# Seven half-width products in place of eight in four down projections of a two-block transformer kernel

## The reference, cut to what matters

```
# block 1
f = rmsnorm(h, norm_ffn_g)
h = h + (silu(f @ w_gate) * (f @ w_up)) @ w_down          # w_down: 2816 x 1024
# block 2
u = causal_dwconv(h2 @ w_ff_up, conv_ff_w, conv_ff_b)      # three taps, per channel
gate, val = split(u, 2)
x = x + (silu(gate) * val) @ w_ff_down                     # w_ff_down: 2816 x 1024
```

## Time and profile before

| | before |
|---|---|
| median of 3 runs | 1555.33 us (1553.41 to 1555.92) |
| span of the profiled execution, first to last instruction | 1553.9 us |
| TensorE matmul busy | 1539.9 us (99%), 7847 matmuls |
| VectorE busy | 747.5 us (48%) |
| ScalarE busy | 395.1 us (25%) |
| GpSimd busy | 905.7 us (58%) |
| mean granted TensorE clock | 0.999 |

### The profile page before, as it was taken

One profiled execution on the slowest core, in us unless ns is written; L12 is line 12 of the kernel. 1 busy time (PEld: TensorE's weight loads), 2 busy tenths in 40 slices (PEclk: granted clock), 3 DMA queues, 4 the chain that ended last, 5 costly groups with the idle time before them and its releaser, 6 DMA issues.

```text
span 1553.9 us, 22779 instructions
## 1 busy us (share of the span) xinstructions
PE 1539.9 (99%) x7847; PEld 1291.7 (83%) x7847; DVE 747.5 (48%) x1157; ACT 395.1 (25%) x757; POOL 905.7 (58%) x536
## 2 busy tenths in 40 slices
PE   8999999999999999999999999999999999999998
PEld 7779999988888888888888888777877888888887
DVE  4157840232335354742343245868567751552456
ACT  4221210233442012210010013456564320220122
POOL 5645556544445667766666666653454666666653
PEclk9999999999999999999999999999999999999999
DMA  6223333322223432333333333322222323333322
GB/s 213 82 72 91 85 93 91 86 68 59 64 68 104 147 95 82 108 94 95 100 100 98 95 88 102 93 70 64 60 67 82 94 81 108 96 98 103 95 81 95
DMA packets 266712, 142.67 MB, mean 92 GB/s; under 512 B 6445, under 2 KB 263749, under 8 KB 266389
## 3 DMA queue, kind: packets, MB, share of 16 engines
q1 hardware_dynamic: 265285, 139.16, 30.5%
q10 hardware_dynamic: 1360, 2.56, 0.4%
HBM read 137.38 MB, written 4.19 MB: 91 GB/s over the span
## 4 chain that ended last, share of the span: by engine, by line
PE 95%; DVE 3%; ACT 1%; issue 1%; DMA 0%; ACTq 0%; DVEq 0%
PE PS L645 74%; PE PS L643 12%; PE PS L872 1%; PE PS L849 1%; PE PS L957 1%; PE PS L797 1%; DVE BL L2051 1%; PE PS L875 0%; PE PS L923 0%; PE PS L848 0%; PE PS L862 0%; DVE L L1881 0%; PE PS L1003 0%; DVE L L1864 0%; ACT SBX L1422 0%
## 5 line engine op out<-in xcount | busy, mean ns | idle before, releaser
L586 POOL TENSOR_TENSOR WL<-RAW,WH 128x1024 fp32r<-128x1024 f32 (+1 forms) x259 | 622.7, 2404 | 21.6
L584 POOL TENSOR_SCALAR WH<-RAW 128x1024 fp32r<-128x1024 f32 (+1 forms) x259 | 280.4, 1083 | 607.6 <-DMA RAW<-in_w_in_dram 257.5
L645 PE MATMUL PS<-BH,WH 128*128 128x512 f32 x928 | 366.6, 395 | 1.2 <-DVE BL L2051 1.1
L645 PE MATMUL PS<-BL,WH 128*128 128x512 f32 x928 | 361.4, 389 | 0.0
L645 PE MATMUL PS<-BH,WL 128*128 128x512 f32 x928 | 361.1, 389 | 0.0
L645 PEld LDWEIGHTS PS<-BH,WH 128*128 128x128 f32 x928 | 174.2, 188 | 42.4 <-issue 4.4
L645 PE MATMUL PS<-AH,WH 128*128 128x512 f32 x528 | 205.9, 390 | 0.0
L645 PE MATMUL PS<-AL,WH 128*128 128x512 f32 x528 | 205.4, 389 | 0.0
L645 PE MATMUL PS<-AH,WL 128*128 128x512 f32 x528 | 205.4, 389 | 0.0
L645 PEld LDWEIGHTS PS<-BH,WL 128*128 128x128 f32 x928 | 174.3, 188 | 37.2 <-issue 1.7
L645 PEld LDWEIGHTS PS<-BL,WH 128*128 128x128 f32 x928 | 174.2, 188 | 36.6
(11 more groups left out here) (334 smaller groups left out, 1817.4 us busy)
## 6 DMA issues: line engine op xcount, KB each, us to landing
RAW<-in_w_in_dram SPq DMA_DIRECT2D x89, 512.0 KB, 3.4
RAW<-in_w_ff_up_dram SPq DMA_DIRECT2D x44, 512.0 KB, 3.6
RAW<-in_w_gate_dram SPq DMA_DIRECT2D x22, 512.0 KB, 3.6
RAW<-in_w_up_dram SPq DMA_DIRECT2D x22, 512.0 KB, 3.6
RAW<-in_w_down_dram SPq DMA_DIRECT2D x16, 512.0 KB, 3.6
RAW<-in_w_ff_down_dram SPq DMA_DIRECT2D x16, 512.0 KB, 3.6
RAW<-in_w_out_dram SPq DMA_DIRECT2D x10, 512.0 KB, 3.7
RAW<-in_w_conv_out_dram SPq DMA_DIRECT2D x8, 512.0 KB, 3.7
```

What stands on the lines that cost most here:

```text
L584: nc.gpsimd.tensor_scalar(WH[:, slot, 0:kc], RAW[:, slot, 0:kc], 1.0, 1.0, ALU.mult, ALU.mult).then_inc(w_hi, 1)
L586: nc.gpsimd.tensor_tensor(WL[:, slot, 0:kc], RAW[:, slot, 0:kc], WH[:, slot, 0:kc].bitcast(F32), ALU.subtract).then_inc(w_ready, 1)
L645: last = mm(bank_of(name, i)[0:rows], w[:, w_at, k, 0:rows], a[:, k, :], start=st, stop=sp_)
```

## The change

It touches `dn0`, `dn1`, `ed0` and `ed1`. Two panels of 8 k and 512 positions are treated as a 2 x 2 block product: the weights are the even and odd k of the first and of the second panel, the activations the even and odd k in the first and second half of the positions (256 columns each). Such a block product can be made of seven block products (Winograd's form of Strassen's method) with sums of the weights and of the activations in front and sums of the results behind. A stage is four such pairs; `product(name, n, q)` is product q of pair n: 4 k x 3 passes = 12 matmuls of 256 columns.

- TensorE: products in the order 1, 5, 2, 6, 4, 7, 3 (`DUO_ORDERS`), the first pair by `duo_stage`: 1, 5, then three of the four k of 2, 6, 3, 4, then their last k, then 7. Products 1, 6 and 7 accumulate in one bank, and VectorE must have read the bank (`evict`) before the next of them starts. `EARLY_PARTS` is 3.
- VectorE: sums of activations while the hidden tiles are made (`even_piece`, `odd_pieces`) and their low parts; three weight sums (`add_second`), a fourth (`add_third`), the low part of the second panel (`low_second`), and seven additions to `H` per pair (`evict`) in place of two. Its order at the end of a gate/up stage is `first_duo`, then `later_duos`.
- ScalarE: all high parts of weights and weight sums, and of the activation pieces.
- GpSimd: per pair the low part of the first panel (`low_first`, 1024 elements per partition), of the first two weight sums (`low_sums`, 1024) and of the third (`low_third`, 512), in the order of `duo_lows`. It makes no high parts in these stages.
- Some per-norm semaphores become one each, and one memset (`XA`) moves to `gu2`.

```diff
+DUO_ORDERS = [(1, 5, 6, 2, 3, 4, 7)] + [(1, 5, 2, 6, 4, 7, 3)] * (DUOS - 1)
+EARLY_PARTS, MADE = 3, 12
 # GpSimd
+            def low_first(name, n):
+                m, s = duo(name, n), duo_slots(name, n)[0]
+                pool.wait_ge(first_hi, m + 1)
+                nc.gpsimd.tensor_tensor(WAL[:, n % 2], RAW[:, s], WH[:, s].bitcast(F32), ALU.subtract).then_inc(first_lo, 1)
+            def low_sums(name, n):
+                pool.wait_ge(duo_added, 4 * duo(name, n) + 4)
+                pool.wait_ge(sums_hi, duo(name, n) + 1)
+                nc.gpsimd.tensor_tensor(WSL[:, n % 2, 0:2], WS[:, n % 2, 0:2], WSH[:, 0:2].bitcast(F32), ALU.subtract).then_inc(sums_lo, 1)
+            def duo_lows(name):
+                low_first(name, 0)
+                low_sums(name, 0)
+                low_third(name, 0)
+                low_first(name, 1)
+                low_sums(name, 1)
+                low_third(name, 1)
+                low_first(name, 2)
+                low_sums(name, 2)
+                low_first(name, 3)
+                low_third(name, 2)
+                low_sums(name, 3)
+                low_third(name, 3)
...
 # TensorE
+            def product(name, n, q, ks=range(4)):
...
+                if ks[0] == 0:
+                    if q in (1, 2):
+                        pe.wait_ge(first_lo, m + 1)
+                    elif q in (5, 6):
+                        pe.wait_ge(sums_lo, m + 1)
+                    elif q == 3:
+                        pe.wait_ge(third_lo, m + 1)
+                    else:
+                        pe.wait_ge(second_lo, m + 1)
+                    if q == 6:
+                        pe.wait_ge(duo_out, 7 * m + DUO_ORDERS[n].index(1) + 1)
+                    elif q == 7:
+                        pe.wait_ge(duo_out, 7 * m + DUO_ORDERS[n].index(6) + 1)
...
+                pe.wait_ge(pieces_lo, MADE * DUO_STAGES.index(name) + 3 * ks[-1] + ARRIVAL[q])
+                for k in ks:
+                    rh, rl = A7H[:, k, PIECES[q]], A7L[:, k, PIECES[q]]
+                    for i, (w, a) in enumerate(((hi, rh), (lo, rh), (hi, rl))):
+                        last = mm(bank, w[:, k], a, start=k == 0 and i == 0 and q not in (6, 7), stop=k == 3 and i == 2, skip_group_check=True)
+            def duo_stage(name):
+                early, rest = range(EARLY_PARTS), range(EARLY_PARTS, 4)
+                product(name, 0, 1)
+                product(name, 0, 5)
+                for q in (2, 6, 3, 4):
+                    product(name, 0, q, early)
+                for q in (6, 2, 3, 4):
+                    product(name, 0, q, rest)
+                product(name, 0, 7)
+                for n in range(1, DUOS):
+                    for q in DUO_ORDERS[n]:
+                        product(name, n, q)
 # ScalarE, end of a gate/up stage
+                    gate_tanh(i, 0)
+                    high_even(g, i, MADE1)
+                    high_first(down, 0)
+                    high_sums(down, 0)
+                    high_second(down, 0)
+                    high_third(down, 0)
+                    gate_tanh(i, 1)
+                    high_first(down, 1)
+                    high_odd(g, i, c0)
+                    duo_highs(down)
 # VectorE
+            def add_second(name, n):
+                m, (s0, s1) = duo(name, n), duo_slots(name, n)
...
+                tt(WS[:, n % 2, 0], RAW[:, s1, 0:KC:2], RAW[:, s1, 1:KC:2], ALU.add).then_inc(duo_added, 1)
...
+                tt(WS[:, n % 2, 1], WS[:, n % 2, 0], RAW[:, s0, 0:KC:2], ALU.subtract).then_inc(duo_added, 1)
+                tt(RAW[:, s1, 0:KC:2], RAW[:, s0, 0:KC:2], RAW[:, s1, 0:KC:2], ALU.subtract).then_inc(duo_added, 1)
+            def low_second(name, n):
...
+                dve.wait_ge(second_hi, duo(name, n) + 1)
+                tt(WL[:, s], RAW[:, s], WH[:, s].bitcast(F32), ALU.subtract).then_inc(second_lo, 1)
+            def first_duo(name, g, i, c0, made):
+                evict(name, 0, 1)
+                odd_pieces(g, i, c0, made)
+                low_odd(g, i)
+                evict(name, 0, 5)
+                low_turned(g, i)
+                add_second(name, 1)
+                evict(name, 0, 6)
+                add_third(name, 1)
+                evict(name, 0, 2)
+                evict(name, 0, 3)
+                evict(name, 0, 4)
+                evict(name, 0, 7)
+                low_second(name, 1)
+            def later_duos(name):
+                for n in range(1, DUOS):
+                    more = n + 1 < DUOS
+                    evict(name, n, 1)
+                    evict(name, n, 5)
+                    if more:
+                        add_second(name, n + 1)
+                    evict(name, n, 2)
+                    evict(name, n, 6)
+                    if more:
+                        add_third(name, n + 1)
+                    evict(name, n, 4)
+                    evict(name, n, 7)
+                    if more:
+                        low_second(name, n + 1)
+                    evict(name, n, 3)
 # VectorE, last two hidden tiles of gu0 and gu1 (i = 3); gv0 and gv1 alike
+                    gated(i, 0, flat_made(MADE1))
+                    even_piece(g, i, c0, MADE1)
+                    low_even(g, i, MADE1)
+                    add_second(down, 0)
+                    add_third(down, 0)
+                    scale_gate(i, 1)
+                    low_second(down, 0)
+                    gated(i, 1, flat_odd(i))
+                    first_duo(down, g, i, c0, MADE1)
+                    later_duos(down)
```

More of the change, by code:

```diff
@@ L68 @@
           ("gv0", 16, "dve"), ("ed0", 8, "dve"), ("gv1", 16, "dve"), ("ed1", 8, "dve"), ("gv2", 12, "dve"), ("ed2", 8, "dve")]
+DUO_STAGES = ["dn0", "dn1", "ed0", "ed1"]
+DUOS = 4
 FIRST, COUNT, OWNER, LETGO = {}, {}, {}, {}
@@ L77 @@
         _n["act"] += _count * 2 // 3
-    else:
+    elif _name not in DUO_STAGES:
         _n[_owner] += _count
@@ L399, in bank_of, with duo, duo_slots, duo_loads @@
             return PJ[:, p % 2, p % 4 // 2 if name in FOUR_DEEP else 0, :]
+        def duo(name, n):
+            return DUOS * DUO_STAGES.index(name) + n
+        def duo_slots(name, n):
+            p = FIRST[name] + 2 * n
+            return p % SLOTS, (p + 1) % SLOTS
+        def duo_loads(name, n):
+            p, twice = FIRST[name] + 2 * n, 2 if name in ("ed0", "ed1") else 0
+            return 16 * (p // SLOTS + 1 + twice), 16 * ((p + 1) // SLOTS + 1 + twice)
+        def duo_bank(name, n, q):
+            if n == 0 and q == 3:
+                return PS[:, 4, 0:HALF_T]
+            which = {1: 0, 6: 0, 7: 0, 5: 1, 2: 2, 3: 2, 4: 3}[q]
+            p = FIRST[name] + which
+            return PS[:, 4 + which if n % 2 else p % 2 * 2 + p % 4 // 2, 0:HALF_T]
+        def duo_products(m, q):
+            return 5 * m + DUO_COUNTED[m % DUOS].index(q) + 1
+        def one(t, i):
+            return t[:, bass.ds(i, 1)].rearrange("p o a n -> p (o a) n")
         EARLY, RSTD_META, RSTD_MIX = PS[:, 3, :], PS[:, 1, 0:META], PS[:, 3, :]
@@ L605, in _ @@
             splits(FIRST["wo2b"], FIRST["gv0"] + 2, twice=2)
-            splits(FIRST["gv0"] + 2, FIRST["ed2"], twice=2)
+            splits(FIRST["gv0"] + 2, FIRST["ed0"], twice=2)
+            duo_lows("ed0")
+            splits(FIRST["gv1"], FIRST["ed1"], twice=2)
+            duo_lows("ed1")
+            splits(FIRST["gv2"], FIRST["ed2"], twice=2)
             splits(FIRST["ed2"], PANELS, GROUPS[2][1], twice=2)
@@ new lines, in evict @@
+            def evict(name, n, q):
+                m, c = duo(name, n), 2 * n
+                if q == 2:
+                    after(name, 2 * n)
+                elif q == 7:
+                    after(name, 2 * n + 1)
+                else:
+                    dve.wait_ge(duo_product, duo_products(m, q))
+                if 7 * m + DUO_ORDERS[n].index(q):
+                    dve.wait_ge(duo_out, 7 * m + DUO_ORDERS[n].index(q))
+                bank = duo_bank(name, n, q)
+                if q == 5:
+                    h = H[:, c:c + 2, HALF_T:T]
+                elif q == 7:
+                    h = H[:, c + 1].rearrange("p (a n) -> p a n", a=2)
+                elif q == 4:
+                    h = H[:, c + 1, 0:HALF_T]
+                else:
+                    h = H[:, c, 0:HALF_T] if q in (1, 2) else H[:, c, HALF_T:T]
+                if q in (5, 7):
+                    bank = bank.unsqueeze(1).to_broadcast([P, 2, HALF_T])
+                stt(out=h, in0=bank, scalar=0.5, in1=h, op0=ALU.mult, op1=ALU.add).then_inc(duo_out, 1)
@@ L1797, in _ @@
+                step(nc.vector.memset(XA[:, :, 0:3], 0.0))
                 with dve.Fori(0, n // 2) as i:
@@ L2090, in _ @@
[L2090 to L2095 removed]
+                        dve.wait_ge(a_lo, i * 2 + (j + A_USE[f"ff{g}"] - 1))
```

394 lines of the change are left out of this document (305 added, 89 removed).

## The result

The changed kernel takes 1587.55 us (median of 4 runs, 1585.80 to 1588.32), the kernel before 1555.5 on the same chip: ratio 1.0208, 95% interval 1.0194 to 1.0222. It is 2.1% slower. The prediction said slower, but 1573 us, with a range that ended at 1582. The profiled execution spans 1584.1 us, 30.2 more than before.

A forecast was written before the change was run, and what follows sets the result against it. TensorE, busy 99% of the span, was taken as the bound. Span 1553.9 + 7.8 (dn0, dn1) + 10.2 (ed0, ed1) = 1571.9, with the median 1.4 above the span: 1573 us, range 1549 to 1582.

The forecast's parts named there:

- What TensorE saves: Four changed stages: 336 half-width matmuls at 0.1205 us make 40.5 us instead of 43.5, saving 3.0 per stage, 12 in all.
- The turns: Changed stages: GpSimd and two-input VectorE instructions exclude each other, filling 9.8 of 10.1 us per pair.
- first rival: Changed stages: the saving stands, turns fall differently and waits are small; 1552 us, or 1542 at 0.113 per matmul; 20%.
- Along a down stage: dn0 and dn1: 40.5 us of matmuls plus listed waits make 47.4 against 43.5, +3.9 per stage, 7.8 for two.
- Item 2: Start of a dn stage: product 6 waits for VectorE's eviction of product 1; 3.1 us lost.
- item 4: dn stage: product 7 waits for eviction of 6, 0.85 us lost; pair 1's product 5 waits for low parts of sums, 0.35.
- item 5: dn stage: product 7 waits behind the next pair's sums and GpSimd's turns, 1.3 us in pair 1, 0.9 in pair 2.
- Items 3: Start of a dn stage: TensorE waits for the odd pieces of the last tile; 0.4 us lost.
- Elsewhere: Outside the four stages: added gate/up VectorE work, up to 4 us per two tiles, loads, semaphores and memset cost nothing.
- the rival of the falling clock: Behind the four long waits: clock falls to 1.2 GHz, 8 us more; 10% beyond 1580, shared with slower half-width matmuls.
- The bound of 0.126: Upper bound in us for a half-width matmul, from 20 in 3.11 less tail; saving then 1.2 per stage, 5 in all.
- The waits are small: Changed stages: the saving stands, dn takes 42.3 us and ed 43.2; 1552 us in all; 20%.

The follow-up runs named there:

- e7: Changed kernel, but GpSimd writes zeros instead of low parts of the first weight panel and the weight sums, leaving those terms out: 1566.02 us, ratio 1.0082.
- e5: Changed kernel with the orders of e2 and e3, and GpSimd instead of VectorE making low parts of the first three odd tiles in gv0, gv1: 1577.04 us, 1.0148.
- e4: Changed kernel with unused matmuls (20, 18, 100, 34) filling TensorE's long waits in dn0, dn1, ed0, ed1: 1582.67 us, ratio 1.0183.
- e1: Seven products in dn0 and dn1 only; ed0 and ed1 as in the kernel before: 1559.99 us, ratio 1.0047.
- e12: e5 with the zeros of e7 in place of GpSimd's low parts of weights: 1559.10 us, ratio 1.0040.
- e13: e12 with the last tile's taps first on ScalarE and VectorE, ahead of high parts and weight sums: 1556.55 us, ratio 1.0020.
- e6: e1 with the early eviction of e3, and ScalarE's high part of pair 1's first panel behind the last tile's pieces: 1559.57 us, ratio 1.0036.
- e8: e5 with ScalarE's high part of pair 1's first panel behind the last tile's pieces in all four stages: 1580.78 us, ratio 1.0176.
- e9: e1 with the early eviction of e3, and the first panel's low part made by VectorE instead of GpSimd: 1557.72 us, ratio 1.0032.
- e10: e9 with the low part of the third weight sum on VectorE too: 1557.96 us, ratio 1.0029.
- e11: e10 with the low parts of the first two sums on VectorE too, so GpSimd makes none in dn0 and dn1: 1553.48 us, ratio 1.0003.
- e2: Changed kernel, but in ed0 and ed1 VectorE scales the gate panel and makes the last even tile's low part ahead of the weight sums: 1587.18 us, 1.0210.
- e3: Changed kernel, but the eviction of the first pair's product 1 stands ahead of the last hidden tile in all four stages: 1587.44 us, ratio 1.0214.
- e14: e11 with the first product's eviction put back behind the last tile's operands: 1551.79 us, ratio 0.9996.

## Why the prediction was right or wrong

- **What bounds the kernel: right.** TensorE, as long as the others deliver.
- **What TensorE saves: right, a little low.** 0.118 per half-width matmul, not 0.1205: 39.7 us a stage, 0.8 less than taken.
- **The turns: right, and the main cause, in block 1 all but alone; their size was taken too low.** e7 takes them away, and 6.0 us of dn0 and 21.2 of the four stages go. The prediction put the forecast "some 10 to 14 us less" without them, though its first rival, in which the turns fall well, is 21 us less.
- **Along a down stage: right for dn.** Item 2 was 3.1 and is 2.6; item 4's product 7 was 0.85 and is 0.86 in dn1, while dn0's slow matmuls take its place; item 5, 1.3 and 0.9, is 1.65 and 0.77. Items 3 and the 0.35 of item 4 didn't appear. The stage came to 46.6 and 46.2 against 47.4. From their first product on, ed0 and ed1 took 47.2 each against 48.6: product 6 lost 1.2 and 0.7 in place of 3.15, product 5 nothing in place of 0.75, and the last k 0.65 as forecast.
- **ed0 and ed1: wrong, +5.1 each forecast, +16.1 and +8.2 measured.** The step that failed is "Elsewhere": "The gate/up stages get up to 4 us per two tiles of VectorE work beside 21.8 us of TensorE ... nothing." All of the excess over the forecast, and more, is here: the first products of ed0 and ed1 start 12.4 and 4.5 us late, where the forecast had only 0.15 each. The 4 us were no less than the work: without a turn a pair takes 2.7 more. But they stood for the sum of durations, with no turns, though the same text had found that two-input instructions of VectorE take turns with GpSimd, and GpSimd makes its low parts all through gv0 too. With turns the first pair gets 7.8 us more, goes from 17.05 to 24.9, and passes TensorE's 21.8. And the room of three panels was thought of as free at the start of the stage; there the norm has already used up most of it (a lead of 3.6 us before, against 15.7 at the end), and what VectorE needs is the 4.7 us per pair by which it caught up. e5 shows the step by the way back: 19.8 us a pair, and ed0 5.9 us shorter. Another 3.9 of the 12.4 us are turns with the low parts of ed0's own weights (L2067, 2.84 us instead of 0.69, is one): by so much its first product comes earlier in e7. Why ed1 starts only 4.5 us late was not taken apart. "It comes with 0.3 of arrears out of the tile before (0.15 taken)" was the same error in the sum for ed.
- **"No clock loss is counted": the clock did fall, and it explains little of the miss.** Behind the 12.2 us wait matmuls are 0.213 apart, granted clock 0.89 over ed0, so the rival of the falling clock had its mechanism, and the time came out on its side of 1580. But all slow distances together are 7.4 us, near its 8, while the late first products alone are 16.9 us and stand ahead of any slow matmul in ed. How much of the 7.4 counts differs: nothing of 1.8 us in e4's trace and 0.3 of 1.1 in dn0 against e1, but between e12 and e13 the windows moved by about as much as the slow matmuls did. The Trainium skill ("TensorE: Matmul & The Clock Gate", HAM oscillation) describes idle stretches after which the clock is low; the rows after agree, with the qualification that 2.43 us of waiting did it in the changed kernel and 2.42 did not in e1.
- **The bound of 0.126** for a half-width matmul does not follow from its row: (3.11 - 0.28) / 20 is 0.14. The forecast did not hang on it, and 0.118 was measured.
- **The rivals.** "The waits are small" is refuted by e1; it would need the turns gone. That the orders tried within GpSimd's share did not get rid of the turns (e6, e8, e9, e10) speaks for "9.8 of 10.1 us leaves no room for order". That the direction came out right is the merit of the turns in block 1; of the 30.1 us, the 24.3 of block 2 were forecast as 10.2.

The sum by the prediction's terms as measured: 1553.9 + 3.1 + 2.7 + 16.1 + 8.2 = 1584.0, the span. What is open: how the last 2.9 us of e13 in ed0 and ed1 could go, what the lower clock costs in the changed kernel, and what moves the stretch between dn1 and ed0 by up to 3.6 us.

## What to carry to other kernels

When work is added to an engine beside the bounding one, redo the sum for every stage that gets some of it, with the turns in it, and ask not whether the engine has room on average but whether it comes into the stage late and how much it wins back per step. Work shared out to a second engine can be worth nothing if both take turns for it: in dn0 VectorE alone did both shares in the same busy time (e11). It is not a rule, since the low parts given to GpSimd in gv0 did help (e5). And a late engine was not helped by reordering its last items (e2, e3, e6); less work, or less waiting inside it, moved the end. Only with the turns gone did an order pay, 0.7 to 0.8 us a stage (e14).
